# Chunk order of the gate and up products, and the place of the gated rows, in the FFN of a two-layer encoder

## What is computed

```python
h = _rmsnorm(x, g_pre_ffn[l]) * (1 + sc2) + sh2
f = (jax.nn.silu(h @ w_gate[l]) * (h @ w_up[l])) @ w_down[l]
x = x + ga2 * _rmsnorm(f, g_post_ffn[l])
```

## Time and profile before

| | |
|---|---|
| runs | 3809.29, 3803.0, 3805.6 us |
| median | 3805.6 us |
| span of the profiled execution | 3804.7 us |
| PE busy in the span | 3386.0 us (89%) |
| DVE, POOL, ACT busy | 1797.6, 1426.3, 1038.8 us |
| FFN on PE, layer 0 and layer 1 | 969.19 to 1986.68 us and 2788.64 to 3782.05 us |

### The profile page before, as it was taken

How to read it: one execution, slowest core, us unless ns; L and a number is a source line. 1 busy time by engine, 2 the same in 40 slices (tenths; PEclk the granted TensorE clock), 3 DMA queues, 4 the chain that set the end, 5 groups by cost and what they waited for, 6 DMA issues and landing times. The chain is left out here.

```text
span 3804.7 us, 48831 instructions
## 1 busy us (share of the span) xinstructions
PE 3386.0 (89%) x19532; PEld 3033.0 (80%) x19532; DVE 1797.6 (47%) x2807; ACT 1038.8 (27%) x2298; POOL 1426.3 (37%) x804
## 2 busy tenths in 40 slices
PE   5998888888999998999988978888899999899997
PEld 2987677767888888888878777776788888888886
DVE  3116777754444534534433156786443453453333
ACT  2323555553100001200014234776320110120001
POOL 2210687810654544444530302000054454455441
PEclk7998899989999999999999988998999999999998
DMA  6205444422322223322222134112232222242222
GB/s 202 71 15 160 143 146 147 150 78 88 101 74 77 72 73 89 99 69 72 73 60 100 55 123 119 29 34 67 76 117 72 67 74 77 72 131 75 72 67 67
DMA packets 397728, 337.90 MB, mean 89 GB/s; under 512 B 107192, under 2 KB 325000, under 8 KB 397504
## 3 DMA queue, kind: packets, MB, share of 16 engines
q1 hardware_dynamic: 249808, 233.18, 20.1%
q10 hardware_dynamic: 147696, 101.61, 9.2%
HBM read 282.87 MB, written 51.87 MB: 88 GB/s over the span
## 5 line engine op out<-in xcount | busy, mean ns | idle before, releaser
L581 POOL TENSOR_SCALAR w_hi<-raw 128x1024 fp32r<-128x1024 f32 (+2 forms) x400 | 458.7, 1147 | 2270.2 <-PE ps L598 2135.0
L583 POOL TENSOR_TENSOR w_lo<-raw,w_hi 128x1024 fp32r<-128x1024 f32 (+2 forms) x400 | 975.4, 2438 | 33.4
L596 PE MATMUL ps<-w_lo,ht_hi 128*128 128x512 f32 (+2 forms) x2040 | 798.5, 391 | 145.8 <-DVE tokm L1685 83.3
L596 PE MATMUL ps<-ht_lo,w_hi 128*128 128x320 f32 x2816 | 873.3, 310 | 4.9 <-DVE ht_lo L1359 3.0
L597 PE MATMUL ps<-ht_hi,w_lo 128*128 128x320 f32 x2816 | 871.6, 310 | 0.0
L598 PE MATMUL ps<-ht_hi,w_hi 128*128 128x320 f32 x2816 | 871.5, 309 | 0.0
L597 PE MATMUL ps<-w_hi,ht_lo 128*128 128x512 f32 (+2 forms) x2040 | 787.1, 386 | 0.0
L598 PE MATMUL ps<-w_hi,ht_hi 128*128 128x512 f32 (+2 forms) x2040 | 784.9, 385 | 0.0
L596 PEld LDWEIGHTS ps<-w_lo,ht_hi 128*128 128x128 f32 x2040 | 397.8, 195 | 232.5 <-DVE tokm L1685 99.0
L596 PEld LDWEIGHTS ps<-ht_lo,w_hi 128*128 128x128 f32 x2816 | 530.0, 188 | 8.1 <-DVE ht_lo L1359 3.8
L597 PEld LDWEIGHTS ps<-ht_hi,w_lo 128*128 128x128 f32 x2816 | 530.0, 188 | 1.6
(11 more groups left out here) (127 smaller groups left out, 3681.2 us busy)
## 6 DMA issues: line engine op xcount, KB each, us to landing
raw<-in_w_gate_dram SPq DMA_DIRECT2D x88, 512.0 KB, 3.8
raw<-in_w_up_dram SPq DMA_DIRECT2D x88, 512.0 KB, 3.8
raw<-in_w_down_dram SPq DMA_DIRECT2D x88, 512.0 KB, 3.5
raw<-in_w_mod_dram SPq DMA_DIRECT2D x80, 512.0 KB, 4.3
x_rows<-tokm ACTq DMA_DIRECT2D x30, 512.0 KB, 5.0
x_old<-x_rows ACTq DMA_DIRECT2D x30, 512.0 KB, 4.3
kv_rows<-stage ACTq DMA_DIRECT2D x20, 512.0 KB, 3.3
tokm<-kv_rows ACTq DMA_DIRECT2D x30, 320.0 KB, 4.1
```

Source lines behind the costliest of these rows:

```text
L581: pool.tensor_scalar(hi, r, 1.0, 0.0, ALU.mult, ALU.add).then_inc(s_whi, 1)
L583: pool.tensor_tensor(lo, r, hi.bitcast(F32), ALU.subtract).then_inc(s_w, 1)
L596: pe.matmul(out, lhs[0], rhs[1], start=first, stop=False)
```

## The change

- PE: a tile runs gate and then up of the first token chunk, then gate and up of the second. The wait for the weights of gate and of up stands ahead of their first chunk.
- DVE writes the gated rows back into the up bank that it reads, and `gated32` is no longer used in the FFN. ACT takes the high part, and DVE the low part, from that bank. So an up group of the next tile waits for the low part of this tile's chunk (semaphore `s_al`), where it waited for the gated product (`s_a32`); the product's own wait for an older low part is gone.
- ACT: silu and high part of the first chunk, then of the second.
- DVE: product and low part of the first chunk, then of the second; after an even tile, three of the 10 additions of the pair before stand ahead of the second chunk's low part and seven behind it (`DOWN_FIRST`).

```diff
+        DOWN_FIRST = 3
                     def gate_up(j):
                         jj = tile_no(l, half, j)
-                        for i, (name, done, read) in enumerate((("w_gate", s_g, s_sil), ("w_up", s_u, s_a32))):
-                            pe.wait_ge(s_w, last_piece[(l, name, half * FT + j)])
-                            for c in range(2):
+                        for c in range(2):
+                            rhs = [[h[:, k, tok0 + c * 320:tok0 + (c + 1) * 320] for h in (ht_hi, ht_lo)] for k in range(KT)]
+                            for i, (name, done, read) in enumerate((("w_gate", s_g, s_sil), ("w_up", s_u, s_al))):
+                                if c == 0:
+                                    pe.wait_ge(s_w, last_piece[(l, name, half * FT + j)])
                                 if jj:
                                     pe.wait_ge(read, 2 * (jj - 1) + c + 1)
                                 for k in range(KT):
...
# ACT
-                        act.activation(act_ring(half, j % 4)[0][:, c * 320:(c + 1) * 320], gated32[:, c, :], ACT.Copy).then_inc(s_ah, 1)
+                        act.activation(act_ring(half, j % 4)[0][:, c * 320:(c + 1) * 320], ps[:, 2 + c, 0:320], ACT.Copy).then_inc(s_ah, 1)
...
                         for c in range(2):
                             silu_chunk(j, c)
-                        for c in range(2):
                             gated_chunk(j, c)
...
# DVE
-                        if n >= 2:
-                            dve.wait_ge(s_al, n - 1)
-                        dve.tensor_tensor(gated32[:, c, :], ps[:, 2 + c, 0:320], stage[:, c * 320:(c + 1) * 320], ALU.mult).then_inc(s_a32, 1)
+                        up = ps[:, 2 + c, 0:320]
+                        dve.tensor_tensor(up, up, stage[:, c * 320:(c + 1) * 320], ALU.mult).then_inc(s_a32, 1)
...
-                        dve.tensor_tensor(lo, gated32[:, c, :], hi.bitcast(F32), ALU.subtract).then_inc(s_al, 1)
+                        dve.tensor_tensor(lo, ps[:, 2 + c, 0:320], hi.bitcast(F32), ALU.subtract).then_inc(s_al, 1)
...
-                            for c in range(2):
-                                gated_product(j, c)
-                            for c in range(2):
-                                gated_low(j, c)
+                            gated_product(j, 0)
+                            gated_low(j, 0)
+                            gated_product(j, 1)
                             if j % 2 == 0 and m:
-                                add_down(m - 1)
+                                add_down(m - 1, 0, DOWN_FIRST)
+                            gated_low(j, 1)
+                            if j % 2 == 0 and m:
+                                add_down(m - 1, DOWN_FIRST, DPP)
```

More of the change, by code:

```diff
@@ L856, in gate_up @@
                                 for k in range(KT):
-                                    rhs = [h[:, k, tok0 + c * 320:tok0 + (c + 1) * 320] for h in (ht_hi, ht_lo)]
-                                    ins = product(ps[:, 2 * i + c, 0:320], [x[:, k, :] for x in w_gu(j, i)], rhs, k == 0, k == KT - 1)
+                                    ins = product(ps[:, 2 * i + c, 0:320], [x[:, k, :] for x in w_gu(j, i)], rhs[k], k == 0, k == KT - 1)
                                 ins.then_inc(done, 1)
@@ L1674, in gated_low, with add_down @@
                         hi, lo = (x[:, c * 320:(c + 1) * 320] for x in act_ring(half, j % 4))
-                        dve.tensor_tensor(lo, gated32[:, c, :], hi.bitcast(F32), ALU.subtract).then_inc(s_al, 1)
-                    def add_down(m):
-                        for n in range(DPP):
+                        dve.tensor_tensor(lo, ps[:, 2 + c, 0:320], hi.bitcast(F32), ALU.subtract).then_inc(s_al, 1)
+                    def add_down(m, n0, n1):
+                        for n in range(n0, n1):
                             t, c = divmod(n, 2)
@@ L1708, in _ @@
                                 split_row_bank(key)
-                    add_down(PAIRS - 1)
+                    add_down(PAIRS - 1, 0, DPP)
             residual(L - 1, 1, NT - 1)
```

## The result

The changed kernel takes 3696.5 us (median of four runs, 3689.7 to 3701.6), the kernel before 3804.3: a ratio of 0.971, 95% interval 0.969 to 0.973. Forecast were 3694, range 3682 to 3716. The profiled execution has a span of 3694.6 us, 110.1 less than before.

The account below looks back on a forecast made before the run. PE bounds the kernel, idling in the FFN on DVE's additions, late behind low parts that POOL lengthens. Gains of 73.2 + 19.8 + 7.6 + 6.9 + 4.0 = 111.5 us from span 3804.7 gave 3694 us, range 3682 to 3716.

Parts of the forecast that it names:

- The timetable of the additions: After an even tile's last up chunk, additions start about 1.4, 2.8, 4.1 and 5.5 us later, leaving PE no wait.
- The 31 and the 5 ordinary waits: PE's waits for additions behind even tiles, five with lower clock, all go: 73.2 and 19.8 us.
- The three long ones: Long `down`s in layer 0's second half, where scaling waits for a store: 2.35, 1.9 and 1.9 us less, 7.6 with clock.
- The last `down` of a half: Four waits for the last low part, 13.3 us in all, fall to 1.6 each: 6.9 us gained.
- The clock behind them: Lower clock in `down` behind the three longer of the half-end waits costs 6.5 us; 4 of these come back.
- One bound: The forecast's own upper bound, 3705 us, with none of the lower-clock time at long waits and ends given back.
- the first rival: Low parts stay long because PSUM doesn't free them from POOL: 3725 us, chance 0.07.
- give way in PSUM: Rival: PE stands still while product, high and low part touch the up banks; up to 253 us, 3947; chance 0.02.
- The new wait in the second half of layer 0: Rival: an up group waits for a low part in tiles 3 and 5, if stores land later: 3702 to 3706; chance 0.06.
- The price of PSUM for DVE: Writing the product to PSUM costs 0.01 us by the rows; product and low part 0.13 us more together by the skill.

Follow-up runs that it names:

- e5: Kernel before, with POOL starting to split a tile's weights at the first gate chunk of the tile ahead, not the last up chunk: 3695.3 us.
- e10: Chunk order alone (rows in SBUF, no addition first), with ACT making the second chunk's high part twice, so its low part comes 0.5 us later: 3806.5 us.
- e2: Changed kernel with the gated rows back in SBUF; chunk order and three additions first stay: 3693.6 us.
- e1: Kernel before with only the place of the gated rows changed, to the up bank in PSUM: 3695.6 us.
- e3: Changed kernel with rows in SBUF and no addition first, so only the chunk order is left: 3703.2 us.
- e6: Changed kernel with the old order on PE (gate of both chunks, then up of both): 3694.4 us.
- e4: Changed kernel with no addition first (DOWN_FIRST = 0), gated rows still in PSUM: 3703.1 us.
- e9: Kernel before with POOL's low part of each FFN weight piece cut into two instructions of 512 columns: 3739.4 us.
- e11: Changed kernel with no addition first, rows in PSUM, and ACT making the second chunk's high part twice: 3710.5 us.

## Why the prediction was right, and where it was not

**The path.** PE's waits behind even tiles, late additions, low parts ahead of them, POOL as their cause: e5 and e10 show this chain from both ends. The timetable of the additions came out too: in the rows above they start 1.4, 2.8, 4.1 and 5.5 us behind the end of the last up chunk (about 1098.4). The two facts on which the forecast rested, 13.63 us for a `down` without a wait and a low part from PSUM that POOL leaves alone, came out at 13.62 and 0.49 us.

**The sum, term by term.** Forecast 111.5 us; the FFN is 61.0 us shorter in layer 0 (1017.5 to 956.5) and 51.4 in layer 1 (993.4 to 942.0), 112.4 together. What lies outside the two FFNs, whose code is the same, took 2.3 us more in this execution, which leaves the 110.1 of the span.

- The 31 and the 5 ordinary waits: 73.2 and 19.8 forecast. All these stretches are 13.62 to 13.63 now, so the terms stand; one of the 31 was only 15.22 long before, 0.8 less.
- The three long ones: 7.6 forecast, 68.4 - 59.55 = 8.9 measured. The first lost 2.3 us, as given; the others 3.2 and 3.3 where I gave 1.9. There the time at the lower clock fell from 6.8 to 3.4 us, for which the sum had 1.5 us in all three together.
- The last `down` of a half: 6.9 forecast for the waits; the wait is 1.6 in all four, as forecast. The clock behind them: 4.0 of 6.5 forecast; the three stretches are 13.75 now (above), at the full clock, 15.36 + 15.32 + 16.63 - 3 x 13.75 = 6.1 measured. The term was too small.
- Not in the sum: the stretch between the last `down` of a first half and the first `down` of the second is longer than before, 53.12 us for 52.31 in layer 0 and 52.97 for 52.27 in layer 1, 1.5 us together. In layer 0 more of it ran at the lower clock (0.90 for 0.93), in layer 1 not (0.94 for 0.93), so the cause stays open.

That the total came within 1 us is luck in part: two terms were 1.3 and 2.1 us too small, and the 0.8 and 1.5 us on the other side nearly make up for it. One bound does not follow from its terms: without the 1.5 and 4.0 us of lower clock the sum gives 3699.5, not the 3705 stated.

**The part that was wrong: how POOL makes a low part long.** I read 481 to 2703 ns in the earlier trace rows as an instruction that is stretched in proportion, and priced the first rival, low parts that stay long behind three additions, at 3725 by a low part of 1.8 us. No low part has such a price of its own: it depends on where it falls between POOL's instructions. e2, the order with low parts from SBUF, measured 3693.6 because there it fell into a gap; that does not say what the rival would have cost outside the gap. The trace of the kernel before already held the answer: in the earlier trace rows the two low parts end at 1106.02, and POOL's low part in that window ends at 1105.66. A median with so wide a range asks what the long ones end with, before it is used as a price. The forecast did not depend on it, since PSUM takes the low part out of the matter either way.

**What each part of the change was worth.** I gave the gain to the three additions first and the shorter low part together. The runs show that place (e1), order with three additions (e2) or a later POOL (e5) each take all of it, e2 by a gap of 0.08 us; that the chunk order alone takes nearly all (e3), but by an accident of 0.3 us (e10); and that beside the place PE's order takes none (e6). Only for the place do the rows show that it holds wherever POOL's instructions fall. Three additions first are worth 3.5 us beside the place (e4, FFN 1902.0 for 1898.5) and 6.8 without it (e3 for e2). In both they lie in the three long stretches, which sum to 62.8 us in e4 and 66.4 in e3, for 59.55 and 59.6 in the changed kernel and e2.

**The rivals.** PE does not give way in PSUM: an ordinary `down` has PE busy for all its 13.62 us beside products, high parts and low parts in the up banks, and the two tiles of gate and up behind it take 28.16 us (1027.92 to 1056.08) where they took 28.15. The new wait in the second half of layer 0 did not come: no up group waits for a low part.

The price of PSUM for DVE was 8 ns on the product and none that shows on the low part: 478 to 494 ns from PSUM (e1), 481 to 495 in the eight rows of the kernel before that POOL did not hold. The Trainium skill, Perfetto Trace Analysis, section Optimizing Scalar/DVE Operations, gives some 125 ns of overhead on PSUM and 60 on SBUF, which makes 65 ns for each of the two by estimate; the trace does not agree, and the time would not have told, as both lie on PE's path at seven places only.

## What to carry to other kernels

When the durations of one instruction shape spread over five times their least, lay its rows beside the other engine's and see with which event the long ones end. A DVE instruction with two SBUF inputs that meets a busy POOL waits for POOL's whole instruction: give it one input in PSUM, start POOL elsewhere, or cut POOL's instructions short; of these only the first does not depend on where the rows happen to fall. A gain from an order should be tried with half a microsecond of delay before it is believed: it may rest on a gap between two instructions of another engine, as e3's did and, by its rows, e2's.

## What the runs showed of the hardware

- A held low part ends 0.33 to 0.36 us behind POOL's instruction in the kernel before, less than its 0.48 us alone. The residual's addition at 1480.77 above ends 1.08 us behind POOL's low part (1483.01), for 1.23 alone. Some 0.14 us of each thus passes while it is held.
- The hold goes by instruction, so two instructions of half the length hold less, although they cost POOL more: 1.30 + 1.30 us for 2.41 (medians of e9 and of the kernel before), and the kernel took 72 us less.
- An instruction with one SBUF input can be held too: the scaling (L1403, one tensor and a column of factors) takes 0.75 us free and 2.05 at 1491.18 above, beside POOL's low part from 1490.31 to 1492.68, while the additions with one input in PSUM take 0.68 to 0.69 us in all 400 cases of the changed kernel.
- The lower clock went with the waits: the 36 ordinary stretches of the changed kernel have none of it, and neither have the three `down`s behind the last tiles of the first three halves, where a wait of 1.6 us is left (the fourth, with residuals between its additions, ran at 0.91 before and after). In the kernel before it came behind all three waits of 3.4 to 4.1 us for a held low part, in e10 behind two of three (4.0 us each; not the 3.3), and in e11 behind two of three waits of 2.06 us.
